# One uncut fp32 product for both halves of the block compression, in place of two products of cut operands

## What is computed

```python
proj = a @ w_in
kv = proj[..., dq:dq + 6 * dkv].reshape(B, S, 6, HK, DH)
k_cmp, v_cmp, k_sel, v_sel, k_win, v_win = [kv[:, :, i] for i in range(6)]
...
def compress(t, w1, w2):
    tb = t[:, blk] + cmp_pos[None, None, :, None, :]
    tb = tb.transpose(0, 1, 3, 2, 4).reshape(B, n_cmp, HK, CMP_BLOCK * DH)
    return jax.nn.silu(tb @ w1) @ w2

kc = compress(k_cmp, cmp_wk1, cmp_wk2)
vc = compress(v_cmp, cmp_wv1, cmp_wv2)
```

## Time and profile before

| what | us |
|---|---|
| median of 3 runs | 902.57 |
| lowest and highest run | 902.1, 903.83 |
| span of the profiled execution | 901.5 |
| TensorE busy in it | 873.2 (97%) |
| VectorE busy | 536.8 (60%) |
| ScalarE busy | 473.9 (53%) |

### The profile page before, as it was taken

The page is one execution under the profiler, slowest core; times in us unless marked ns, Lnnn a source line. Parts: engine busy times, 40 slices in busy tenths (PEclk is TensorE's granted clock), DMA queues, the critical chain, the costliest instruction groups (busy, mean ns, idle before and its releaser), DMA issues. The chain is left out here.

```text
span 901.5 us, 12726 instructions
## 1 busy us (share of the span) xinstructions
PE 873.2 (97%) x4345; PEld 710.1 (79%) x4345; DVE 536.8 (60%) x1119; ACT 473.9 (53%) x819; POOL 60.0 (7%) x134
## 2 busy tenths in 40 slices
PE   6999999999999999989999999999999999999995
PEld 5898666778888888778887888888788788888874
DVE  5878776587645545685555535545555865555533
ACT  7676666665444444455445544445554644444331
POOL 3000038020000000110000000000001100000002
PEclk9999999999999999999999999999999999999998
DMA  7666100454656456347555015555204376645611
GB/s 251 206 203 222 47 2 1 140 165 157 217 187 222 150 189 226 98 151 241 178 182 158 1 48 173 184 168 187 82 1 141 118 232 199 220 154 188 217 47 48
DMA packets 90107, 135.20 MB, mean 150 GB/s; under 512 B 6304, under 2 KB 55504, under 8 KB 90064
## 3 DMA queue, kind: packets, MB, share of 16 engines
q1 hardware_dynamic: 89392, 132.53, 45.9%
q0 software_dynamic: 576, 2.10, 0.7%
q10 hardware_dynamic: 96, 0.02, 0.0%
HBM read 133.59 MB, written 1.05 MB: 149 GB/s over the span
## 5 line engine op out<-in xcount | busy, mean ns | idle before, releaser
L948 DVE TENSOR_TENSOR w_lo<-w_raw,w_hi 128x1024 fp32r<-128x1024 f32 x248 | 301.3, 1246 | 111.5 <-ACT w_hi L524 107.7
L1377 PE MATMUL ps<-w_hi,xt_hi 128*128 128x512 f32 x784 | 314.5, 401 | 2.1 <-DVE xt_lo L978 1.9
L1377 PE MATMUL ps<-w_hi,xt_lo 128*128 128x512 f32 x784 | 307.4, 392 | 0.0
L1377 PE MATMUL ps<-w_lo,xt_hi 128*128 128x512 f32 x784 | 306.9, 391 | 0.0
L524 ACT ACTIVATE w_hi<-w_raw 128x1024 fp32r<-128x1024 f32 x248 | 252.2, 1054 | 42.5 <-DMA w_raw<-in_ffn_w_gu 19.6
L1377 PEld LDWEIGHTS ps<-w_hi,xt_hi 128*128 128x128 f32 x784 | 148.4, 189 | 32.4 <-DVE xt_lo L978 2.7
L1377 PEld LDWEIGHTS ps<-w_hi,xt_lo 128*128 128x128 f32 x784 | 148.3, 189 | 31.4
L1377 PEld LDWEIGHTS ps<-w_lo,xt_hi 128*128 128x128 f32 x784 | 148.7, 190 | 28.3
L776 ACT ACTIVATE st_hi<-ps 128x256 fp32r<-128x256 f32 x44 | 16.8, 383 | 112.6 <-PE ps L1386 112.6
L1377 PE MATMUL ps<-w_hi,st_hi 128*128 128x512 f32 x176 | 69.0, 392 | 2.9 <-DVE st_lo L1240 2.8
L502 POOL TENSOR_TENSOR h<-h,tmp 128x512 f32<-128x512 f32 x16 | 24.1, 1527 | 714.6 <-DVE tmp L1216 714.6
(11 more groups left out here) (176 smaller groups left out, 825.5 us busy)
## 6 DMA issues: line engine op xcount, KB each, us to landing
w_raw<-in_ffn_w_gu SPq DMA_DIRECT2D x88, 512.0 KB, 4.7
w_raw<-in_dil_w_in SPq DMA_DIRECT2D x72, 512.0 KB, 4.0
w_raw<-in_ffn_w_down SPq DMA_DIRECT2D x44, 512.0 KB, 4.0
w_raw<-in_nsa_w_in SPq DMA_DIRECT2D x20, 512.0 KB, 4.6
w_raw<-in_nsa_w_o SPq DMA_DIRECT2D x8, 512.0 KB, 4.4
w_raw<-in_dil_w_o SPq DMA_DIRECT2D x8, 512.0 KB, 4.0
w_raw<-in_nsa_cmp_wk SPq DMA_DIRECT2D x4, 512.0 KB, 5.2
w_raw<-in_nsa_cmp_wv SPq DMA_DIRECT2D x4, 512.0 KB, 4.0
```

Of the source, the lines that this page charges most:

```text
L948: dve.tensor_tensor(w_lo[:, n.slot, c:c + 1024], w_raw[:, n.raw, c:c + 1024], w_hi[:, n.slot, c:c + 1024].bitcast(F32), ALU.subtract)\
L1377: ins = pe.matmul(o, s, m, start=start, stop=stop)
```

## The change

**The product.** `compress` is called once. For each of the 16 slices of 128 rows it issues two uncut fp32 matmuls: keys with `w1_k` into partitions 0 to 63 of bank 3, values with `w1_v` into partitions 64 to 127 of the same bank. The stationary operand has 64 columns in each. `turn_kv(2, ...)` and `turn_kv(3, ...)` now stand together behind it.

**The operands.** The blocks of keys and values are both written to one fp32 tile `tb`; `block_hi` and `block_lo` go. `w1` is no longer cut: SP loads it straight into the memory of ring places 0 and 1, the keys' in that of `w_hi`, the values' in that of `w_lo`, once pieces 0 and 1 are used. The four pieces of `w1` leave the sequence of splits; two numbers remain for the two ring places, and `split_no` keeps the counts of halves right. All later pieces have numbers smaller by two.

**The order on the other engines.** ScalarE and VectorE lose four splits each. ScalarE's splits of the first query pieces, 8 and 9 now, stand in front of and behind `turn_kv(1, 0, 4)`; the exponential is one instruction of 128 partitions, and so is VectorE's product into `hid_r`.

```diff
-N_CMPKV, N_SEL, N_WIN, N_WK1, N_WV1, N_Q, N_NSAO = 0, 2, 4, 6, 8, 10, 14
-N_FFN0 = 18
+N_CMPKV, N_SEL, N_WIN, N_W1, N_Q, N_NSAO = 0, 2, 4, 6, 8, 12
+N_FFN0 = 16
...
+    @property
+    def split_no(self):
+
+        return self.n0 - 2 if self.n0 >= N_Q else self.n0
...
+        slot_w1 = N_W1 % RING * PIECE * 4
+        w1_k = sb("w1_k", [P, 2, PIECE], at=at_hi + slot_w1)
+        w1_v = sb("w1_v", [P, 2, PIECE], at=at_lo + slot_w1)
...
-            def cmp_w1(n, w):
-                wv = w[0].rearrange("(k p) c -> p k c", p=P)
+            def cmp_w1():
+
                 for half in range(2):
-                    load(n + half, *[(wv[:, 8 * half + k:8 * half + k + 4, :], 256 * k,
-                                      [[256, 4], [1, 256]]) for k in (0, 4)])
+                    sp.wait_ge(piece_used, Piece(N_W1 + half).used() - RING)
+                    for w, dst in ((nsa_cmp_wk1, w1_k), (nsa_cmp_wv1, w1_v)):
+                        wv = w[0].rearrange("(k p) c -> p k c", p=P)
+                        for k in (0, 4):
+                            sp.dma_start(view(dst, half * PIECE + 256 * k, [[256, 4], [1, 256]]),
+                                         wv[:, 8 * half + k:8 * half + k + 4, :])\
+                              .then_inc(w1_loaded[half], 16)
...
-            split(6)
             proj_evac(kv_sel)
-            block_hi(0)
             turn_kv(0, 0, 7)
-            split(7, (0,))
-            block_hi(1)
-            split(7, (1,))
 
             proj_evac(kv_win)
             turn_kv(0, 1, 2)
+            proj_evac(kv_win)
             split(8)
-            proj_evac(kv_win)
+            turn_kv(1, 0, 4)
             split(9)
-            turn_kv(1, 0, 4)
+
+            act.wait_ge(hid_sum, 1)
+            act.activation(e_hid[:, :], bank(3, 0, 256), ACT.Exp, scale=-1.0).then_inc(hid_exp, 1)
+            turn_kv(1, 1, 5)
             split(10)
-            split(11)
...
-            def compress(kv, n, b):
+            def compress():
 
 
                 pe.wait_ge(tb_ready, 2)
                 for kt in range(16):
-                    p, c = Piece(n + kt // 8), (kt % 8) * 256
-                    if kt % 4 == 0:
-                        pe.wait_ge(lo_ready, p.halves(kt % 8 // 4 + 1))
-                    ins = three(bank(b, 0, 256), tb_hi[:, kt, :, :].rearrange("p a b -> p (a b)"),
-                                tb_lo[:, kt, :, :].rearrange("p a b -> p (a b)"),
-                                w_hi[:, p.slot, c:c + 256], w_lo[:, p.slot, c:c + 256], kt == 0, kt == 15)
+                    half, c = kt // 8, kt % 8 * 256
+                    if kt % 8 == 0:
+                        pe.wait_ge(w1_loaded[half], 64)
+                    for kv, w1 in enumerate((w1_k, w1_v)):
+                        ins = pe.matmul(ps[64 * kv:64 * kv + 64, 3, 0:256],
+                                        tb[:, kt, kv, :, :].rearrange("p a b -> p (a b)"),
+                                        w1[:, half, c:c + 256], start=kt == 0, stop=kt == 15)
                     if kt == 7:
                         ins.then_inc(piece_used, 1)
                 ins.then_inc(hid_sum, 1)
...
-            compress(0, N_WK1, 3)
+            compress()
             pe.wait_ge(pair_dve, 1)
             turn_kv(2, 0, 4)
-            pe.wait_ge(pair_dve, 2)
-            compress(1, N_WV1, 6)
             pe.wait_ge(pair_act, 2)
             turn_kv(3, 1, 5)
             nsa_gemm(6, N_Q)
```

More of the change, by code:

```diff
@@ L107, in halves @@
     def halves(self, k):
-        return self.it * (2 * RING) + 2 * self.n0 + k
+        return self.it * (2 * RING) + 2 * self.split_no + k
     def used(self):
@@ L143, in build @@
         w_raw = sb("w_raw", [P, RAW, PIECE])
+        at_hi = place[0]
         w_hi = sb("w_hi", [P, RING, PIECE], F32R)
+        at_lo = place[0]
         w_lo = sb("w_lo", [P, RING, PIECE], F32R)
+        slot_w1 = N_W1 % RING * PIECE * 4
+        w1_k = sb("w1_k", [P, 2, PIECE], at=at_hi + slot_w1)
+        w1_v = sb("w1_v", [P, 2, PIECE], at=at_lo + slot_w1)
         h = sb("h", [P, MT, D])
@@ L309, in build @@
         pair_act, pair_dve = sem("pair_act"), sem("pair_dve")
-        tb_f_ready, tb_hi_ready, tb_ready = sem("tb_f_ready"), sem("tb_hi_ready"), sem("tb_ready")
+        tb_ready = sem("tb_ready")
+        w1_loaded = [sem(f"w1_loaded{half}") for half in range(2)]
         gate_zero, gate_sum, gate_copied = sem("gate_zero"), sem("gate_sum"), sem("gate_copied")
@@ L370, in _ @@
                 sp.dma_start(dst, w[0].rearrange("(k p) d -> p k d", p=P)).then_inc(w2_loaded, 16)
-            def cmp_w1(n, w):
-                wv = w[0].rearrange("(k p) c -> p k c", p=P)
+            def cmp_w1():
                 for half in range(2):
-                    load(n + half, *[(wv[:, 8 * half + k:8 * half + k + 4, :], 256 * k,
-                                      [[256, 4], [1, 256]]) for k in (0, 4)])
+                    sp.wait_ge(piece_used, Piece(N_W1 + half).used() - RING)
[5 more added lines that the diff above has]
+                              .then_inc(w1_loaded[half], 16)
             chunk(Piece(N_WIN), w_in, 2048)
-            cmp_w1(Piece(N_WK1), nsa_cmp_wk1)
-            cmp_w1(Piece(N_WV1), nsa_cmp_wv1)
+            cmp_w1()
             chunk(Piece(N_Q), w_in, 0)
@@ L685, in _ @@
             proj_evac(q_rows)
-            split(13)
+            split(11)
             proj_evac(q_rows)
-            split(14, (0,))
+            split(12, (0,))
             turn_q(0, 0, 7, 2)
@@ L695, in _ @@
             ins.then_inc(kc_out, 1)
-            split(14, (1,))
+            split(12, (1,))
             proj_evac(q_rows)
-            split(15, (0,))
+            split(13, (0,))
             turn_q(0, 1, 4, 5)
-            split(15, (1,))
+            split(13, (1,))
             cmp_exp(0)
@@ L1073, in _ @@
             blocks(0)
-            block_lo(0)
             dve.wait_ge(pair_dve, 2)
             blocks(1)
-            split(7, (0,))
-            block_lo(1)
-            split(7, (1,))
             rope(0, 5, stage_nsa, 0, 2 * HK, 0)
+            rope(0, 6, stage_nsa, 1, 2 * HK, 1)
             split(8)
-            rope(0, 6, stage_nsa, 1, 2 * HK, 1)
             split(9)
-            split(10)
-            split(11)
-            dve.wait_ge(hid_exp, 2)
+            dve.wait_ge(hid_exp, 1)
             link(dve.tensor_scalar(e_hid[:, :], e_hid[:, :], 1.0, None, ALU.add))
             link(dve.reciprocal(e_hid[:, :], e_hid[:, :]))
[L1090 to L1093, removed]
+            dve.tensor_tensor(hid_r[:, :], bank(3, 0, 256), e_hid[:, :], ALU.mult).then_inc(hid_ready, 1)
             dve.wait_ge(gate_exp, 2)
@@ L1098, in _ @@
             link(dve.reciprocal(flat, flat))
-            split(12)
+            split(10)
             dve.wait_ge(hid_psum, 1)
@@ L1106, in _ @@
             rope(0, 7, stage_rot, 0, 8, 0)
-            split(13)
+            split(11)
             rope(0, 8, stage_rot, 1, 8, 1)
-            split(14)
+            split(12)
             dve.wait_ge(kc_out, 1)
@@ L1147, in _ @@
             rope(0, 9, stage_rot, 0, 8, 0)
-            split(15)
+            split(13)
             cmp_scores(0)
@@ L1203, in _ @@
                     ot_lo((s - 15) // 8)
-            split(16)
+            split(14)
             ot_lo(HK - 1)
```

30 lines of the change are left out of this document (6 added, 24 removed).

## The result

The changed kernel takes 913.61 us (median of 4 runs, 912.6 to 914.73), against 902.74 (4 runs of the kernel before on the same chip): a ratio of 1.0121 [1.0107, 1.0135]. It is **slower by 1.2%**, where 0.4% faster was forecast, and the time lies far outside the range. In some executions, of the unchanged kernel too, the clock stood at half for 20 to 31 us in the dilated attention, which costs 9 to 14 us (by their times, 7 of 24 executions of e4 and e8 had one, 3 of 9 of e3 and e5, none of 17 of e1 and e7, and one of some 40 of the kernel before); the profiles of e4, e5, e6 and e8 hold such a stretch, and the ratios of e3, e4 and e8 still include some of these executions.

The account below looks back on a forecast made before the run. TensorE, busy 97%, was taken to bound the kernel. Product 6 could start 4.5 us earlier; waits for piece 9 and the hidden rows left 3.6, so 902.57 - 3.6 = 899.0 us, range 897.0 to 901.2.

Parts of the forecast that it names:

- What bounds the kernel: Whole kernel: TensorE, busy 97% of the span, sets the time; a change counts by its effect on TensorE's sequence and waits.
- What goes, what comes: Compression on TensorE: 12.31 us go; 64 uncut instructions at 0.215 us come, overlapped to 6.9 us; product 6 4.5 us earlier.
- The halves side by side: Compression: keys' and values' matmuls, in different partition halves, overlap throughout, taking 6.9 us where one stream takes 13.8.
- The new waits: TensorE waits 0.6 us in product 6 for piece 9, and 0.9 us for the hidden rows, whose transposes come 3.6 us earlier.
- no new wait: Rival at product 6 and hidden rows: splits keep up with TensorE; hidden transposes 5.3 us earlier, 897.3 us; chance 0.07.
- From there on the order of the engines is the old one ... no new wait: Behind the hidden rows' transposes: no further gain and no new wait; product 7 and all behind it move by 3.6 us.
- The clock: Around the change the granted clock is 1.00, the level of 2.4 GHz; no change of clock was counted.
- From span to median: Whole run: the median lies 1.07 us above the profiled span of 901.5 us, and this was kept for the changed kernel.
- The rivals: Compression: one stream (0.10), half an overlap (0.10), no new wait (0.07); gain from ScalarE and VectorE work alone was excluded.
- one stream: Rival in the compression: alternating matmuls run in order, 13.8 us in place of 6.9, giving 905.9 us, slower; chance 0.10.

Follow-up runs that it names:

- e4: e1 with ScalarE's split of piece 9 and the exponential moved ahead of both copies into `k_z`; 899.44 us, ratio 0.9976.
- e8: e4 run once more, unedited; 898.79 us, ratio 0.9981.
- e3: e1 with all the keys' compression instructions issued first, then all the values'; median 909.84 us, ratio 1.0097.
- e5: e1 with keys and values as one stream of 128 weight columns, into banks 3 and 6, without halves; 907.9 us, ratio 1.0053.
- e1: The changed kernel with the compression's matmuls issued through the helper that pays the owed `piece_used` increment; 900.5 us, ratio 0.9976.
- e7: e1 run once more, unedited; 900.17 us, ratio 0.9970.
- e6: The kernel before, unedited, profiled once more; its profiled execution took 912.97 us.
- e2: The kernel before with only the `piece_used` increment owed at the start of the keys' compression dropped; 915.6 us, ratio 1.0138.

## Why the prediction was wrong, point by point

- **What bounds the kernel: right.** TensorE's sequence sets the time; every term below was read from it and came back in it.
- **What goes, what comes: right.** Forecast 0.215 us an instruction, measured 0.216 (e3, e5); forecast 7.06 us to the transposes and 7.82 to product 6, measured 7.06 and 7.91. In the 7.06 the first step is 0.267 and the last, to the transposes, 0.32, so entering and leaving cost 0.15 (forecast 0.16). In e1, product 6 comes 4.27 us earlier, forecast 4.5.
- **The halves side by side: right, and now by trial.** One stream costs 6.0 us (e3) and 6.8 us (e5) more, forecast 6.9. The rule of the Trainium skill (TensorE: Matmul & The Clock Gate, Part 3, The mechanism), by which the loads of 137 ns would be exposed, doesn't hold here: 64 of them beside matmuls in the same rows cost nothing. The same section also lets a load into the background weight buffer be pulled ahead of matmuls under way, which the prediction left out; no run here tells which buffer was used.
- **The new waits: right.** The profile lists 0.42 us on `w_lo` and 0.57 on `hid_r` in e1. Read from starts, as the forecast was, they are 0.58 (the matmul ahead starts at 63.54; forecast 0.6) and 0.73 (66.98; forecast 0.9). The hidden rows' transposes come 3.54 and 3.82 us earlier (e1, e7), forecast 3.6; what the copy ahead of split 9 costs is 1.3 to 1.6 us (e8), as the rival "no new wait" had it (1.7).
- **"From there on the order of the engines is the old one ... no new wait": this step failed.** The order of instructions is the old one; what each waits for is not. I counted durations, transfers and waits of the instructions that the change moves, and not the increments that the removed ones carried. The line `ins = pe.matmul(...)` stood in the diff, and beside it `three(...)` that it replaces. The one question "who adds to `piece_used` for piece 5 now?" would have found it. It cost 11.8 us at the passages (-2.02 to +9.74), more than three times the gain.
- **The clock: a small miss.** I counted no change. In after it fell to half for some 3 us at 26 us, behind a wait for `gw_lo`, and cost 1.5 us; this is not due to the lost count, which comes later (and e2 has none of it), and it didn't return in e1, e3, e5, e7 and e8. It fell again behind the passages, which is within the 11.8.
- **From span to median: a term too small.** With the count paid the spans of the traces are 3.8 and 4.0 us shorter (901.5 to 897.7 and 897.5), the medians only 2.2 and 2.7 (902.68 - 900.5, 902.91 - 900.17). The record has the span of every execution of the experiments and explains this. The 41 of the kernel before each took 1.67 to 1.77 us outside the span (e2 and e6 too), the 17 of e1 and e7 2.04 to 2.16, and the other kernels with the new compression 2.04 to 2.20. So some 0.4 us belong to the changed kernel and fall outside the span; where they come from stays open. The 1.07 us that I kept set one execution's span, 901.5, against the median of others; the median spans of before are 901.0 and 901.2. The traces of e1 and e7 are short ones in their turn (median spans 898.4 and 898.05), so the gain in median spans is 2.6 and 3.1 us.
- **The rivals.** None was this one. All of them concerned the compression; I had none for what the change does far behind it. My chance of 0.1 for slower rested on "one stream" alone.

As a forecast of the change as it was meant, 899.0 us stands against 900.5 and 900.17: right in sign, 1.2 to 1.5 us too low, within the range.

## What to carry to other kernels

When a change takes instructions away or issues them by another route, list for each semaphore who adds to it, piece by piece, before and after, and not only what each new instruction costs: one increment lost here made a ring of six places one of five, and was paid 100 us later. The sign of it in a profile is the splits' row in ScalarE's list of waits: 86.5 us for the matrix engine in 21 waits, where it was 2.8 in two, and a passage between layers that is late while all ahead of it runs earlier. A product with 64 columns of weights does best when two of them write different halves of the output and change at every instruction: in one stream the same work took 6.8 us longer, and two long rows, one after the other, overlap only where they meet.

## What the runs showed of the hardware

**How far matmuls run ahead.** With the halves alternating, pairs start within 0.01 us. With the halves in two rows of 32, the second row starts four instructions before the first ends, and no sooner (e3). The half that is free is not used further ahead than that.

**Weight loads of 64 columns.** 133 to 137 ns each, in both halves, beside a pace of 0.216 us a pair. The rows of after, shortest, median and longest in ns:

```profile
L1467 PE MATMUL ps<-w_k,tb x32: 379/379/430, 54.5 to 61.3; 128*64 128x256 f32 x32
L1467 PEld LDWEIGHTS ps<-w_k,tb x32: 133/137/137, 54.5 to 61.1; 128*64 128x64 f32 x32
```

**The clock at half early in the run.** TensorE waits for `gw_lo` at 25 us in every kernel. Where that wait was 2.0 us (after) and 1.8 (e4) the clock was 0.5 for some 3 us behind it; where it was 0.5 to 1.5 (the others) it stayed at 1.00. The length of a wait alone does not settle it: behind the wait of 2.5 us at the second passage of after it stayed at 1.00. The wait in after, and the stretch behind it beside the same one in e1 (PE, PEld, DVE, ACT, POOL busy, clock, DMA share, GB/s):

```profile
24.98 0.39 PE L1361 MATMUL ps<-xt_hi,gw_hi 128*128 128x256 f32 x1 [2.02 <-DVE gw_lo L996]
```

```profile
26.00:29.00 3.00, 3.00 (x17) 3.00 (x16) 2.86 (x7) 1.51 (x2) 0.00 (x0) 0.52 0.37 140
```

```profile
26.00:29.00 3.00, 3.00 (x27) 3.00 (x26) 2.86 (x7) 1.88 (x2) 0.00 (x0) 1.00 0.50 190
```

At half clock, the level of 1.2 GHz, 17 matmuls are listed where 27 are at 2.4 GHz.

**The clock at half in the dilated attention.** It stood at 0.50 for 20.5 us in e4, e5 and e6, and for 30.7 in e8, with TensorE busy throughout. In all four the fall begins 2.2 to 2.4 us behind a wait of TensorE, 0.96 us (e4, e6) or 1.01 us (e5, e8), which ends at the first matmul on `qk_t` of one of the layer's two stretches of attention; the expectation of e8, which says that no wait is in front, is wrong there. Every other profile has both of these waits, at the same length and without a fall. The wait in e6, where the clock is 1.00 up to 641.8 and 0.50 from there on, and the same one in the first trace:

```profile
639.44 1.87 PE L1799 MATMUL ps<-qk_t 64*128 64x256 f32 x11 [0.96 <-ACT v_dil L855]
```

```profile
638.67 2.53 PE L1799 MATMUL ps<-qk_t 64*128 64x256 f32 x18 [0.96 <-ACT v_dil L855]
```

A fall of 20.5 us cost 9.2 to 9.3, the one of 30.7 cost 13.9. The same ten microseconds in e6 and in the first trace of the same kernel:

```profile
650.00:660.00 10.00, 10.00 (x38) 7.86 (x38) 3.23 (x10) 3.11 (x7) 0.00 (x0) 0.50 0.00 0
```

```profile
650.00:660.00 10.00, 10.00 (x69) 8.10 (x69) 4.95 (x17) 4.49 (x12) 0.00 (x0) 1.00 0.01 2
```

Why an execution falls there and the next does not is open; the unchanged kernel has it too, so it is not the change's alone.
